# A second late row buffer, another schedule for the late rows, exchanged gate buffers, and second operands split one product later

## The chip, the core and the metric

One core of a Trainium2 chip runs the whole program. The metric is the device time of one execution in microseconds (us); lower is better. The profiled execution has records of every engine: PE (TensorE) for matmuls, PEld for its weight loads, DVE (VectorE), ACT (ScalarE), POOL (GpSimd) and SP (SyncE); SPq stands for the DMA instructions that SP issues.

## The reference, cut to what matters

The reference is one inference step of a decoder layer over 2048 prompt tokens and 8 sample requests. Three kinds of attention (retention, latent attention, attention to a memory) and a gate all take their inputs from one projection, and only that projection is touched here:

```python
def project(h, pos, norm_g, w_in, qnorm_g, w_uq, w_uk, kvnorm_g):
    B, T, _ = h.shape
    z = rms_norm(h, norm_g) @ w_in
    rq, rk, rv, cq, ckv, kpe, mq, gate = _split_cols(z, IN_SIZES)
    rq = rope(rq.reshape(B, T, RET_HEADS, HEAD_DIM), pos)
    rk = rope(rk.reshape(B, T, RET_HEADS, HEAD_DIM), pos) * (HEAD_DIM ** -0.5)
...
```

The hidden width is 1024; `w_in` has 4288 columns, the last 1536 of them the gate's.

## The kernel before

**Stripes and products.** The projection is cut into 15 stripes of `w_in` columns, at most 512 wide (`STRIPES`). Stripes 0 to 8 take the first 1024 tokens (the rows x 0 to 7 of 128 tokens each), stripes 9 to 14 the second 1024 (the eight "late rows"); the gate's columns of the second half come last, in 24 tiles outside the stripes. A stripe is multiplied by a seven-product scheme: x and w are split in quarters, sums and differences of quarters are made, and seven products ("11", "12", "s1", "s2", "s4", "s3", "22") are recombined. Stripes 0 and 10 are narrow and take four products. Each product runs in three passes of fp32r matmuls over a high and a low part of each operand. The products are numbered through as g, from 0 to 98. Stripe 3 begins at g = 18, stripe 4 at 25, stripe 5 at 32, stripe 6 at 39, stripe 7 at 46, stripe 8 at 53, stripe 9 at 60, and the last stripe, 14, at 92. `base` below is 25. Stripes 5 to 8 are of kind "T", products of 24 matmuls of 512 columns.

**Engines.** Every engine runs its own loop over g, written out by hand, and the order inside one g is the order of its instructions. PE: at the last product of a stripe the sample rows' partial products (L1190, `row_parts`), at its second their sum (L1199), then the late rows' transposes (L1087, `late_turn`), then the product (L1162, L1170). ACT: one evacuation of a product at most (L695), the high part of the weights of product g + 2 (L682, `weight_high`, which waits for product g - 1), late rows. DVE: recombination (L902, L1005), the low part of the weights of g + 2 (L868), sums of weights (L880 to L891), rotations (L920 to L927, `rotate`), late rows (L815, L854 to L857). SP issues the stores of results (L494) and the late rows' DMAs; POOL issues the weight loads (L398, L410, L420) and computes the late rows' roots (L388, L390).

**Late rows.** The eight late rows are normalised, transposed and spilled to DRAM during stripes 4 to 8, two to a stripe. For row y: load into the one buffer `row_x` (L474), sum of squares on ACT (L618), root on POOL, scale on DVE (L815), eight transposes in two parts on PE (L1087) into one PSUM bank, each part copied by ACT into `late_x` (L638). PE's second part waits for ACT's copy of the first. After a pair of rows, SP stores four quarters of `late_x` (L477, counted by `late_out`), DVE makes four sums in place (L854 to L857), which waits for `late_out`, and SP stores the four sums (L477, counted by `sums_out`). The copy of the next pair's first part waits for `sums_out`. Only one buffer: the load of the next row waits until the last one is transposed. With p the first product of the pair's stripe, the steps are, for its first row: square at p, scale at p + 1, transposes at p + 2 and p + 3; for its second: load and square at p + 4, scale at p + 5, transposes at p + 6 and p + 7; spill at p + 8, sums at p + 9. The next pair's first row is loaded behind that spill, at p + 8, which is one past the next stripe's first product, where ACT's loop already stands at its square.

```python
def late_turned(y, part):
    act.wait_ge(xT_ps, TURNS + 2 * y + part + 1)
    if y >= 2 and part == 0:
        act.wait_ge(sums_out, 64 * (y // 2))
...
    act.copy(late_x[:, y % 2, part, :, :], turn_bank[0]).then_inc(late_ok, 1)
```

**Second operands.** During stripe 8 and the first product of stripe 9 SP loads the seven operands of the second half, 1 MB each, from DRAM over the old ones, each as soon as stripe 8 has used it (L480); "11" waits for `late_out`, "s1" for `sums_out`. ACT makes the high parts (L661, `second_high`) and DVE the low parts (L848, `low_part`).

**Gate tiles.** For n from 0 to 23 a tile of 24 matmuls (L1211) is copied to `stage` by ACT (even n) or DVE (odd n) and stored by SP. For every four tiles one stripe of gate weights is split by ACT (L692) and DVE (L953, `gate_low`) into `wh` and `wl`. Of the four result buffers c[0] to c[3] of 4 KB each, the stage takes c[0] and c[1] and the second `wl` takes c[2] and c[3]; so `gate_low(1)` waits until the last stripe's results 2 and 3 are stored (`c_out`), and the first copies to the stage until 0 and 1 are. Between the tiles runs the preparation of the sample requests: on DVE `sample.vector(0)` (L3268 to L3274 and L3240 to L3244) stands behind `gate_low(1)`, and PE's `sample.tensor(1)` (L3461, L3465), which stands behind the second tile, waits for it. SP issues the sample's 16 first DMAs (from L3115 on) ahead of the last result store (L494, `store(LAST, 3)`).

Of the kernel before, what the change touches and what calls it, by code (L numbers as in the profile page):

```python
# [21 lines left out]
F32R = mybir.dt.float32r  # L22
# [134 lines left out]

def product_plan():
# [8 lines left out]
    for n, s in enumerate(rotary):  # L167
        for z, after in enumerate((2, 3, 5, 7, 8, 8, 11, 11)):
            pieces.setdefault(first[s] + after, []).append((n, z))
# [4 lines left out]
def project(nc, t, hold, tail):  # L174
# [6 lines left out]
    with ExitStack() as ctx:  # L181
# [37 lines left out]
        row_x = at(right(4 * KB), "row_x", [P, D])  # L219
# [6 lines left out]
        if high.at < low.at:  # L226
# [16 lines left out]
        wl = [at(w_at[1], "wl0", [P, KD, SW], F32R), at(c_at + 8 * KB, "wl1", [P, KD, SW], F32R)]  # L243
        stage = at(c_at, "stage", [P, 2, 2, BIG])
# [6 lines left out]
         gate_out, row_x_in, late_ok, late_out, late_sum, sums_out, chain,  # L251
# [3 lines left out]
            "gate_out row_x_in late_ok late_out late_sum sums_out chain "  # L255
# [7 lines left out]
        op_in = {n: r.sem(f"op_in_{n}") for n in FULL}  # L263
        rope_ok = [r.sem(f"rope_ok{j}") for j in range(2)]
# [44 lines left out]
        def pair_at(j):  # L309

            return first[SPREAD + j]
# [37 lines left out]
        def stage_free(eng, n):  # L349
            if n // 2 >= 2:  # L350
                eng.wait_ge(st_out[n // 2 % 2], 16 * (n // 4))
            else:
                eng.wait_ge(c_out[n // 2], 16 * stored_before(LAST + 1, n // 2))
# [14 lines left out]
        with nc.Block() as block:  # L368
            @block.gpsimd
            def _(pool):  # L370
# [63 lines left out]
                for s in range(len(STRIPES)):  # L434
                    j = s - SPREAD
                    if 0 <= j < LATE_BLOCKS // 2:
                        late_root(2 * j)
                    if 1 <= s < LAST:
                        load_second(s + 1)
                    if 0 <= j < LATE_BLOCKS // 2:  # L440
                        late_root(2 * j + 1)
                    if s + 2 <= LAST:
                        load_first(s + 2)
                load_gate(0)
# [6 lines left out]
            def _(sp):  # L451
# [19 lines left out]
                def load_late(y):  # L471
                    if y:
                        sp.wait_ge(xT_ps, TURNS + 2 * y)
                    sp.dma_start(row_x[:, :], x_rows[KD + 4 * (y % 2) + y // 2]).then_inc(row_x_in, 16)  # L474
# [51 lines left out]
                for g, (s, i) in enumerate(where):  # L526
# [21 lines left out]
                    for n, turned in enumerate(rotary):  # L548
                        for z, after in enumerate((4, 8, 9, 12)):
# [8 lines left out]
                    for j in range(LATE_BLOCKS // 2):  # L558
                        if g == pair_at(j) + 4:
                            load_late(2 * j + 1)  # L560
                        if g == pair_at(j) + 8:
                            sp.wait_ge(late_ok, 4 * j + 4)
                            for a, n in enumerate(("11", "12", "21", "22")):
                                spill(n, j, late_x[:, a // 2, a % 2, :, :]).then_inc(late_out, 16)
                            if j + 1 < LATE_BLOCKS // 2:
                                load_late(2 * j + 2)
                        if g == pair_at(j) + 9:
                            sp.wait_ge(late_sum, j + 1)
                            for n, of in (("s1", late_x[:, 1, 1, :, :]), ("s2", late_x[:, 0, 0, :, :]), ("s4", late_x[:, 0, 1, :, :]),
                                          ("s3", late_x[:, 1, 0, :, :])):  # L570
                                spill(n, j, of).then_inc(sums_out, 16)
# [33 lines left out]
            def _(act):  # L605
# [7 lines left out]
                def late_squared(y):  # L613
                    act.wait_ge(row_x_in, 16 * (y + 1))
# [3 lines left out]
                    act.activation(late_squares[:, :], row_x[:, :], ACT.Square, accum_out=total[:, FRONT + 2 + y:FRONT + 3 + y]).then_inc(sum_ok, 1)  # L618
# [3006 lines left out]
```

## Time and profile before

| | us |
|---|---|
| median of 3 executions | 2212.25 |
| lowest and highest | 2205.29, 2212.87 |
| the profiled execution's own time | 2208.42 |
| its span, first to last instruction | 2206.6 |
| PE busy | 2031.9 (92%) |
| DVE busy | 1447.5 (66%) |
| ACT busy | 764.2 (35%) |
| mean granted TensorE clock, share of full | 0.971 |

Times in rows of the trace are counted from the span's start. The projection up to product 98 ends near 698, the gate tiles near 880, and the attentions and the merge follow. A timeline row is the start, the duration, the engine, the line, the operation with what it writes and reads, and how many were merged in it; in brackets stands how long the engine had sat idle before it and who released it. Matmuls overlap, so a row can end after the next one starts.

### The profile page before, as it was taken

What the parts mean: (1) busy time and instruction counts of PE and PEld (TensorE: products, weight loads), DVE (VectorE), ACT (ScalarE), POOL (GpSimd) and SP (SyncE); (2) the same over time, 40 slices, a digit from 0 to 9 for tenths busy, and PEclk for the clock granted to TensorE, in tenths of its full rate; (3) what the DMA queues carried; (4) which work ended last, traced back from release to release, by engine and by line L of the source; (5) the groups of instructions that cost most, each with busy time, mean ns of one, the idle gap of its engine ahead of it and who ended that gap; (6) DMA issues with size and microseconds to landing.
All of it is one profiled execution on the core that took longest, in us unless ns stands there. A gap on an engine that the chain in (4) does not pass through costs nothing. (4 is left out here: it accounts for less than half of the span.)

```text
span 2206.6 us, 46989 instructions
## 1 busy us (share of the span) xinstructions
PE 2031.9 (92%) x19805; PEld 1711.8 (78%) x19805; DVE 1447.5 (66%) x2517; ACT 764.2 (35%) x1488; POOL 272.5 (12%) x368
## 2 busy tenths in 40 slices
PE   7999988899998789899989999899899999989998
PEld 6899866689996677677767777678788888768886
DVE  3757544464773441898889999677677777655555
ACT  5323322342332111243334333454444545421110
POOL 1000000000000100222222222112302200000000
PEclk9999999999999899899999999899999999999999
DMA  7332444473244663999999999689948542345542
GB/s 241 120 97 78 144 134 134 126 247 101 88 132 152 215 224 144 377 376 369 366 351 386 377 365 374 207 291 347 328 95 167 94 84 99 124 127 161 172 143 86
DMA packets 205013, 454.78 MB, mean 206 GB/s; under 512 B 15328, under 2 KB 114688, under 8 KB 195600
## 3 DMA queue, kind: packets, MB, share of 16 engines
q0 software_dynamic: 49552, 252.12, 34.6%
q1 hardware_dynamic: 155264, 199.81, 27.3%
q8 instruction: 150, 2.46, 0.4%
q14 instruction: 47, 0.39, 0.1%
HBM read 350.00 MB, written 101.69 MB: 205 GB/s over the span
## 5 line engine op out<-in xcount | busy, mean ns | idle before, releaser
L2813 PE MATMUL sa_ps_s<-sa_turned,keep_q 128*32 128x128 f32 x5120 | 184.4, 278 | 26.2 <-DVE sa_turned L2569 21.3
L1170 PE MATMUL pj_ps<-pj_w,pj_xh_s 128*128 128x256 f32 (+1 forms) x1088 | 192.7, 280 | 0.0
L868 DVE TENSOR_TENSOR pj_w<-pj_raw,pj_w 128x1024 fp32r<-128x1024 f32 (+1 forms) x86 | 102.7, 1194 | 119.0 <-ACT pj_w L682 118.8
L1170 PE MATMUL pj_ps<-pj_w,pj_xh 128*128 128x256 f32 (+1 forms) x960 | 173.8, 284 | 3.7 <-DVE pj_kT L862 3.7
L2813 PEld LDWEIGHTS sa_ps_s<-sa_turned,keep_q 128*32 128x32 f32 x5120 | 136.4, 111 | 51.5 <-DVE sa_turned L2569 28.5
L1170 PEld LDWEIGHTS pj_ps<-pj_w,pj_xh_s 128*128 128x128 f32 x1088 | 166.9, 189 | 0.3 <-issue 0.3
L2569 DVE STREAM_TRANSPOSE sa_turned<-sa_nat 128x2048 f32<-128x2048 f32 x64 | 146.9, 2295 | 18.3 <-DMA sa_kp<-cache_kpe,keep_index 18.3
L1170 PEld LDWEIGHTS pj_ps<-pj_w,pj_xh 128*128 128x128 f32 x960 | 150.2, 193 | 9.3 <-issue 5.5
L1170 PE MATMUL pj_ps<-pj_w,pj_xl_s 128*128 128x256 f32 (+1 forms) x544 | 152.4, 280 | 0.0
L2569 DVE STREAM_TRANSPOSE sa_turned<-keep_nat 128x2048 f32<-128x2048 f32 x64 | 146.9, 2295 | 7.6 <-PEq L85 4.8
L1923 DVE TENSOR_TENSOR la_pl<-la_ps_p,la_ph 128x512 fp32r<-128x512 f32 (+1 forms) x144 | 88.4, 657 | 72.1 <-ACT la_ph L1969 72.1
L1170 PE MATMUL pj_ps<-pj_w,pj_xl 128*128 128x256 f32 (+1 forms) x480 | 135.7, 283 | 0.0
L682 ACT CAST pj_w<-pj_raw 128x1024 fp32r<-128x1024 f32 (+1 forms) x86 | 87.9, 1026 | 137.0 <-PE pj_ps L1170 84.1
L1960 ACT ACTIVATE la_row<-la_row,la_soft 128x128 f32<-128x128 f32 (+7 forms) x64 | 77.3, 1208 | 127.6 <-DVE la_soft L1910 127.6
L695 ACT ACTIVATE pj_c<-pj_ps 128x1024 f32<-128x1024 f32 x52 | 53.3, 1026 | 179.5 <-PE pj_ps L1170 97.2
L1162 PE MATMUL pj_ps<-pj_xh_s,pj_w 128*128 128x512 f32 x320 | 108.2, 421 | 2.8 <-ACT pj_c L695 2.8
L1170 PEld LDWEIGHTS pj_ps<-pj_w,pj_xl_s 128*128 128x128 f32 x544 | 102.9, 189 | 0.0
L1902 DVE CUSTOM_DVE_ANT_0 la_row<-la_ps_s,begin_causal 128x512 f32<-128x512 f32 (+3 forms) x160 | 92.2, 605 | 9.2 <-PE la_ps_s L2026 9.2
L1170 PEld LDWEIGHTS pj_ps<-pj_w,pj_xl 128*128 128x128 f32 x480 | 92.9, 194 | 0.0
L1969 ACT CAST la_ph<-la_ps_p 128x512 fp32r<-128x512 f32 (+1 forms) x144 | 74.3, 565 | 39.4 <-PE la_ps_p L2039 38.5
L1162 PEld LDWEIGHTS pj_ps<-pj_xh_s,pj_w 128*128 128x128 f32 x320 | 64.7, 204 | 18.6 <-issue 3.2
L2039 PE MATMUL la_ps_p<-begin_ident,la_row 128*128 128x128 f32 x544 | 74.0, 276 | 4.1 <-DVE la_row L1917 4.1
(516 smaller groups left out, 4995.4 us busy)
## 6 DMA issues: line engine op xcount, KB each, us to landing
pj_raw<-w_in POOLq DMA_DIRECT2D x32, 1024.0 KB, 6.3
s_zn<-pj_c SPq DMA_DIRECT2D x32, 512.0 KB, 2.9
rm_z<-s_zn SPq DMA_DIRECT2D x16, 768.0 KB
s_zt<-pj_c SPq DMA_DIRECT2D x20, 512.0 KB, 2.8
s_x<-pj_late_x SPq DMA_DIRECT2D x32, 256.0 KB
s_k<-lp_st SPq DMA_DIRECT2D x16, 512.0 KB, 8.3
s_v<-lp_st SPq DMA_DIRECT2D x32, 256.0 KB, 4.8
s_qn<-lp_st SPq DMA_DIRECT2D x16, 512.0 KB, 5.5
```

The source lines that it names most:

```text
L682: act.copy(w_parts(g)[0], w_source(s, i)).then_inc(w_hi, 1)
L695: return act.activation(c[:, q, :, :], bank_pair(b), ACT.Copy, scale=factor(s))
L868: dve.tensor_tensor(lo, w_source(s, i), hi, ALU.subtract).then_inc(w_lo, 1)
L1162: mm = pe.matmul(ps[:, bank + u, :], wt[:, b, k, u * P:(u + 1) * P], of[a][:, k, :], start=opens and (k, a, b) == (0, 0, 0), stop=k == HAL ...
L1170: mm = pe.matmul(ps[:, bank + u, x2 * SW:x2 * SW + w], of[a][:, k, rows_at:rows_at + P], wt[:, b, k, 0:w], start=opens and (x2, k, a, b) = ...
L1902: dve.tensor_tensor_reduce(out=row[:, s, q, c * P:(c + w) * P], in0=ps_s[:, (at + n) % 3, 0:w * P], in1=m, scale=1.0, scalar=-3.0e38, op0= ...
L1923: dve.tensor_tensor(pl[:, n % RING, 0:w], ps_p[:, n % RING, 0:w], ph[:, n % RING, 0:w], ALU.subtract).then_inc(pl_ok, 1)
L1960: act.activation(row[:, s, q, 0:n], row[:, s, q, 0:n], ACT.Exp, bias=soft[:, s, q, 1:2], scale=MLA_SCALE, accum_out=soft[:, s, q, 2:3]).th ...
L1969: act.copy(ph[:, n % RING, 0:w], ps_p[:, n % RING, 0:w]).then_inc(ph_ok, 1)
L2039: mm = pe.transpose(ps_p[:, n % RING, at:at + P], of, ident[:, :])
L2569: dve.transpose(turned[:, s, a:z, :, :].rearrange("p c x q -> p x c q"), of.rearrange("p x (c q) -> p x c q", q=QR)).then_inc(t_ok, 1)
L2813: mm = pe.matmul(ps_s[j * QR:(j + 1) * QR, s, 0:TQ * QR], q32[:, u, c, :], turned[:, s, c, j * TQ:(j + 1) * TQ, :].rearrange("p x q -> p ( ...
```

## The change

The late rows get a second buffer, `row_x1`, in 4 KB of the table of rotations; the squares' scratch has the first 2 KB of the same table. Odd rows use it. The first load into it waits until stripe 3's rotations are done, later loads until the row two before is transposed. A function `late_plan()` gives for each row, as distances from product 25, when it is loaded, squared, scaled and first transposed; the second part is transposed one product later. The rows (load, square, scale, transpose) are (0, 0, 2, 3), (4, 6, 7, 8), (5, 9, 10, 12), (10, 11, 12, 14), (14, 15, 16, 18)... in steps of six products per pair: row 4 is (14, 15, 16, 18), row 5 (16, 17, 18, 20), row 6 (20, 21, 22, 24) and row 7 (22, 23, 24, 26). The spills are at 9, 15, 21 and 27, the sums at 10, 16, 22 and 28, where before they were at 8, 15, 22, 29 and 9, 16, 23, 30. Stripe 3's last two pieces of rotation move from 11 products after its first to 9 and 10, and its last store from 12 to 11. POOL's loads and roots are put in order of g. The high parts of the second operands move from 2 to 8 after stripe 8's first product to 3, 4, 6, 7, 8, 9 and 10, and the low parts are one product behind them each. In the gate tiles, the stage and the second `wl` exchange places, and the waits with them. Nothing is computed differently. Blank context and the renaming of the semaphore are left out below, and eight columns of indentation.

```diff
@@ -155,6 +155,17 @@
+def late_plan():
+    plan = [(0, 0, 2, 3), (4, 6, 7, 8)]
+    for j in range(1, LATE_BLOCKS // 2):
+at = 12 + 6 * (j - 1)
+plan.append((5 if j == 1 else at - 4, at - 3, at - 2, at))
+plan.append((10 if j == 1 else at - 2, at - 1, at, at + 2))
+    return plan
...
@@ -165,7 +176,7 @@
-for z, after in enumerate((2, 3, 5, 7, 8, 8, 11, 11)):
+for z, after in enumerate((2, 3, 5, 7, 8, 8) + ((11, 11) if s + 1 in rotary else (9, 10))):
...
@@ -216,7 +227,7 @@
-row_x = at(right(4 * KB), "row_x", [P, D])
+row_x = [at(right(4 * KB), "row_x0", [P, D]), at(rot_at + 2 * KB, "row_x1", [P, D])]
...
@@ -240,19 +251,19 @@
-wl = [at(w_at[1], "wl0", [P, KD, SW], F32R), at(c_at + 8 * KB, "wl1", [P, KD, SW], F32R)]
-stage = at(c_at, "stage", [P, 2, 2, BIG])
+wl = [at(w_at[1], "wl0", [P, KD, SW], F32R), at(c_at, "wl1", [P, KD, SW], F32R)]
+stage = at(c_at + 8 * KB, "stage", [P, 2, 2, BIG])
...
@@ -261,6 +272,7 @@
+row_x_in = [r.sem(f"row_x_in{j}") for j in range(2)]
...
@@ -306,9 +318,18 @@
-def pair_at(j):
-    return first[SPREAD + j]
+late = late_plan()
+base = first[SPREAD]
+late_loaded, late_squares_at, late_scaled, late_turned_at = [{base + x[n]: y for y, x in enumerate(late)} for n in range(4)]
+late_second_at = {g + 1: y for g, y in late_turned_at.items()}
+late_spilled = {g: y // 2 for g, y in late_second_at.items() if y % 2}
+late_summed = {g + 1: j for g, j in late_spilled.items()}
+second_at = {first[SECOND - 1] + after: y for y, after in enumerate((3, 4, 6, 7, 8, 9, 10))}
+def faded_after(n):
+    return (4, 8, 9, 12 if rotary[n] + 1 in rotary else 11)
...
@@ -350,7 +371,7 @@
-        eng.wait_ge(c_out[n // 2], 16 * stored_before(LAST + 1, n // 2))
+        eng.wait_ge(c_out[2 + n // 2], 16 * stored_before(LAST + 1, 2 + n // 2))
...
@@ -431,16 +452,13 @@
-        for s in range(len(STRIPES)):
-            j = s - SPREAD
-            if 0 <= j < LATE_BLOCKS // 2:
-                late_root(2 * j)
-            if 1 <= s < LAST:
+        for g, (s, i) in enumerate(where):
+            if i == 3 and 1 <= s < LAST:
                 load_second(s + 1)
-            if 0 <= j < LATE_BLOCKS // 2:
-                late_root(2 * j + 1)
-            if s + 2 <= LAST:
+            if i == len(names_of(s)) - 1 and s + 2 <= LAST:
                 load_first(s + 2)
+            if g in late_squares_at:
+                late_root(late_squares_at[g])
...
@@ -469,9 +487,11 @@
-            if y:
-                sp.wait_ge(xT_ps, TURNS + 2 * y)
-            sp.dma_start(row_x[:, :], x_rows[KD + 4 * (y % 2) + y // 2]).then_inc(row_x_in, 16)
+            if y == 1:
+                sp.wait_ge(rope_ok[1], 8)
+            elif y >= 2:
+                sp.wait_ge(xT_ps, TURNS + 2 * (y - 1))
+            sp.dma_start(row_x[y % 2][:, :], x_rows[KD + 4 * (y % 2) + y // 2]).then_inc(row_x_in[y % 2], 16)
...
@@ -546,7 +566,7 @@
-                for z, after in enumerate((4, 8, 9, 12)):
+                for z, after in enumerate(faded_after(n)):
...
@@ -555,20 +575,19 @@
-            for j in range(LATE_BLOCKS // 2):
-                if g == pair_at(j) + 4:
-                    load_late(2 * j + 1)
-                if g == pair_at(j) + 8:
-                    sp.wait_ge(late_ok, 4 * j + 4)
-                    for a, n in enumerate(("11", "12", "21", "22")):
-                        spill(n, j, late_x[:, a // 2, a % 2, :, :]).then_inc(late_out, 16)
-                    if j + 1 < LATE_BLOCKS // 2:
-                        load_late(2 * j + 2)
-                if g == pair_at(j) + 9:
-                    sp.wait_ge(late_sum, j + 1)
-                    for n, of in (("s1", late_x[:, 1, 1, :, :]), ("s2", late_x[:, 0, 0, :, :]), ("s4", late_x[:, 0, 1, :, :]),
-                                  ("s3", late_x[:, 1, 0, :, :])):
-                        spill(n, j, of).then_inc(sums_out, 16)
+            if g in late_loaded and late_loaded[g]:
+                load_late(late_loaded[g])
+            if g in late_spilled:
+                j = late_spilled[g]
+                sp.wait_ge(late_ok, 4 * j + 4)
+                for a, n in enumerate(("11", "12", "21", "22")):
+                    spill(n, j, late_x[:, a // 2, a % 2, :, :]).then_inc(late_out, 16)
+            if g in late_summed:
+                j = late_summed[g]
+                sp.wait_ge(late_sum, j + 1)
+                for n, of in (("s1", late_x[:, 1, 1, :, :]), ("s2", late_x[:, 0, 0, :, :]), ("s4", late_x[:, 0, 1, :, :]),
+                              ("s3", late_x[:, 1, 0, :, :])):
+                    spill(n, j, of).then_inc(sums_out, 16)
...
@@ -611,11 +630,11 @@
-            act.wait_ge(row_x_in, 16 * (y + 1))
+            act.wait_ge(row_x_in[y % 2], 16 * (y // 2 + 1))
...
-            act.activation(late_squares[:, :], row_x[:, :], ACT.Square, accum_out=total[:, FRONT + 2 + y:FRONT + 3 + y]).then_inc(sum_ok, 1)
+            act.activation(late_squares[:, :], row_x[y % 2][:, :], ACT.Square, accum_out=total[:, FRONT + 2 + y:FRONT + 3 + y]).then_inc(sum_ok, 1)
...
@@ -760,26 +779,17 @@
-                for z, after in enumerate((4, 8, 9, 12)):
+                for z, after in enumerate(faded_after(n)):
...
-            for j in range(LATE_BLOCKS // 2):
-                if g == pair_at(j) + 7:
-                    late_turned(2 * j + 1, 1)
-            for j in range(LATE_BLOCKS // 2):
-                if g == pair_at(j):
-                    late_squared(2 * j)
-                if g == pair_at(j) + 2:
-                    late_turned(2 * j, 0)
-                if g == pair_at(j) + 3:
-                    late_turned(2 * j, 1)
-                if g == pair_at(j) + 4:
-                    late_squared(2 * j + 1)
-                if g == pair_at(j) + 6:
-                    late_turned(2 * j + 1, 0)
-            if first[SECOND - 1] + 2 <= g < first[SECOND - 1] + 9:
-                y = g - first[SECOND - 1] - 2
-                second_high(FULL[y], y)
+            if g in late_turned_at:
+                late_turned(late_turned_at[g], 0)
+            if g in late_second_at:
+                late_turned(late_second_at[g], 1)
+            if g in late_squares_at:
+                late_squared(late_squares_at[g])
+            if g in second_at:
+                second_high(FULL[second_at[g]], second_at[g])
...
@@ -812,7 +822,7 @@
-            dve.scalar_tensor_tensor(row_x[:, :], row_x[:, :], stat[:, (PAIRS + y) % 2, 1, 0:1], gain[:, :], ALU.mult, ALU.mult)\
+            dve.scalar_tensor_tensor(row_x[y % 2][:, :], row_x[y % 2][:, :], stat[:, (PAIRS + y) % 2, 1, 0:1], gain[:, :], ALU.mult, ALU.mult)\
...
@@ -948,7 +958,7 @@
-                for q in (2, 3):
+                for q in (0, 1):
...
@@ -1031,16 +1041,13 @@
-            for j in range(LATE_BLOCKS // 2):
-                if g == pair_at(j) + 1:
-                    late_scale(2 * j)
-                if g == pair_at(j) + 5:
-                    late_scale(2 * j + 1)
-                if g == pair_at(j) + 9:
-                    late_sums(j)
-            for y, after in enumerate((3, 4, 5, 8, 9, 10, 11)):
-                if g == first[SECOND - 1] + after:
-                    low_part(FULL[y], len(FULL) + y + 1, xr[FULL[y]])
+            if g in late_scaled:
+                late_scale(late_scaled[g])
+            if g in late_summed:
+                late_sums(late_summed[g])
+            if g - 1 in second_at:
+                y = second_at[g - 1]
+                low_part(FULL[y], len(FULL) + y + 1, xr[FULL[y]])
...
@@ -1084,7 +1091,7 @@
-                mm = pe.transpose(turn_bank[0][:, k, :], row_x[:, d:d + P], ident[:, :])
+                mm = pe.transpose(turn_bank[0][:, k, :], row_x[y % 2][:, d:d + P], ident[:, :])
...
@@ -1231,16 +1238,10 @@
-            for j in range(LATE_BLOCKS // 2):
-                if g == pair_at(j) + 7:
-                    late_turn(2 * j + 1, 1)
-            for j in range(LATE_BLOCKS // 2):
-                if g == pair_at(j) + 2:
-                    late_turn(2 * j, 0)
-                if g == pair_at(j) + 3:
-                    late_turn(2 * j, 1)
-                if g == pair_at(j) + 6:
-                    late_turn(2 * j + 1, 0)
+            if g in late_turned_at:
+                late_turn(late_turned_at[g], 0)
+            if g in late_second_at:
+                late_turn(late_second_at[g], 1)
...
```

## Rows read from the trace of the kernel before

**Rows 1.** PE's waits, 225 to 480 us: waited for, us, times, longest.

```profile
PE pj_ps L1087 <- ACT pj_late_x L638: 18.2, 3, 6.9
PE pj_ps L1087 <- DVE pj_row_x L815: 12.0, 4, 3.8
PE pj_ps L1162 <- ACT pj_c L695: 2.8, 1, 2.8
```

**Rows 2.** PE's waits, 697 to 785 us, the same columns.

```profile
PE pj_ps L3461 <- DVE sp_queries L3272: 11.2, 1, 11.2
PE pj_ps L3435 <- DVE sp_weights L3251: 9.2, 1, 9.2
PE pj_ps L3465 <- DVE pj_late_row L3244: 0.6, 1, 0.6
```

**Rows 3.** Windows: stretch, length, busy by engine, PE clock, DMA share, GB/s.

```profile
264.00:478.00 214.00, 183.66 (x827) 141.37 (x826) 98.99 (x93) 63.89 (x73) 11.81 (x20) 0.92 0.50 160
295.00:297.00 2.00, 2.00 (x6) 1.56 (x5) 2.00 (x2) 0.37 (x1) 0.00 (x0) 0.50 0.78 221
659.10:698.00 38.90, 38.88 (x170) 31.38 (x168) 18.58 (x16) 12.72 (x11) 0.89 (x1) 1.00 0.35 122
703.00:713.00 10.00, 7.58 (x34) 5.95 (x32) 0.00 (x0) 0.59 (x1) 0.00 (x0) 1.00 1.04 359
722.00:730.00 8.00, 7.39 (x24) 5.86 (x24) 5.44 (x14) 0.36 (x2) 1.57 (x3) 0.58 0.41 128
```

**Rows 4.** PE's timeline around the late rows, undisturbed steps and the first stall.

```profile
231.75 0.66 PE L1087 MATMUL pj_ps<-pj_ident,pj_row_x 128*128 128x128 f32 x4 [2.69 <-DVE pj_row_x L815]
312.98 1.91 PE L1190 MATMUL pj_ps<-pj_raw,pj_xsT 128*8 128x256 f32 x32
314.82 0.66 PE L1087 MATMUL pj_ps<-pj_ident,pj_row_x 128*128 128x128 f32 x4
315.24 0.71 PE L1162 MATMUL pj_ps<-pj_xh,pj_w 128*128 128x512 f32 x2
326.80 1.02 PE L1199 MATMUL pj_ps<-pj_rows,pj_parts 128*8 128x512 f32 x2
327.76 0.73 PE L1162 MATMUL pj_ps<-pj_xh,pj_w 128*128 128x512 f32 x2
```

**Rows 5.** Timelines of SP, ACT and DVE around the third pair.

```profile
341.90 3.31 SPq L477 DMA_DIRECT2D s_x<-pj_late_x  x4
349.47 0.59 ACT L638 COPY pj_late_x<-pj_ps 128x512 f32<-128x512 f32 x1 [14.73 <-DMA s_x<-pj_late_x]
341.18 0.69 DVE L857 TENSOR_TENSOR pj_late_x<-pj_late_x 128x512 f32<-128x512 f32 x1
330.80 1.06 ACT L618 ACTIVATE pj_late_squares<-pj_row_x 128x1024 bf16<-128x1024 f32 x1 [8.28 <-DMA pj_row_x<-x_prompt]
```

**Rows 6.** DVE timeline ahead of the first transposes: low part, then scale.

```profile
225.05 1.23 DVE L868 TENSOR_TENSOR pj_w<-pj_raw,pj_w 128x1024 fp32r<-128x1024 f32 x1 [3.11 <-ACT pj_w L682]
230.42 1.28 DVE L815 SCALAR_TENSOR_TENSOR pj_row_x<-pj_row_x,pj_stat,pj_gain 128x1024 f32<-128x1024 f32 x1
```

**Rows 7.** Timelines of DVE, PE and SP at the gate tiles.

```profile
699.27 1.22 DVE L902 SCALAR_TENSOR_TENSOR pj_c<-pj_ps,pj_c 128x1024 f32<-128x1024 f32 x1
714.91 2.29 DVE L953 TENSOR_TENSOR pj_wl<-pj_raw,pj_wh 128x2048 fp32r<-128x2048 f32 x1 [14.42 <-DMA s_zt<-pj_c]
721.57 0.47 DVE L3274 SCALAR_TENSOR_TENSOR sp_ckvx<-sp_first,sp_stat,sp_ring 8x256 f32<-8x256 f32 x1
710.20 0.39 PE L1211 MATMUL pj_ps<-pj_xl,pj_wh 128*128 128x512 f32 x1
723.27 0.80 PE L1211 MATMUL pj_ps<-pj_xh,pj_wh 128*128 128x512 f32 x1
706.07 0.43 SPq L494 DMA_DIRECT2D s_zt<-pj_c  x1
731.46 1.18 PE L3472 MATMUL pj_ps<-sp_weights,sp_cqT 128*32 128x192 f32 x24
```

More of the change, by code:

```diff
@@ L250, in project @@
          decay_in, parts_in, rot_in, mm_ok, ev_act, ev_dve, w_hi, w_lo, sum_w, pr_ok, clear_ok, row4_ps, row4_ok, row_ps, row_ok, row_out,
-         gate_out, row_x_in, late_ok, late_out, late_sum, sums_out, chain,
+         gate_out, late_ok, late_out, late_sum, sums_out, chain,
          e1, e2, e3, e4, e5, e6, e7, e7b, p0, p1, g_hi, g_lo, g_ok, g_act, g_dve) = [r.sem(n) for n in (
@@ L254, in project @@
             "decay_in parts_in rot_in mm_ok ev_act ev_dve w_hi w_lo sum_w pr_ok clear_ok row4_ps row4_ok row_ps row_ok row_out "
-            "gate_out row_x_in late_ok late_out late_sum sums_out chain "
+            "gate_out late_ok late_out late_sum sums_out chain "
             "e1 e2 e3 e4 e5 e6 e7 e7b p0 p1 g_hi g_lo g_ok g_act g_dve").split()]
```

## The prediction, made before the change was run

> **What bounds the kernel now.** I read the page first: PE is busy for 92% of the span, so only what makes PE wait, or lowers its clock, can count. Next I read PE's waits in the projection. Between 225 and 480 us PE stands for 33 us, and 30 of it ahead of the late rows' transposes, L1087: 18.2 in three waits for ACT's copy, 12.0 in four for DVE's scale [rows 1]. The window view gives the same from outside: of the 214.0 us of products 32 to 59 PE is busy for 183.66, at a mean granted clock of 0.92, while in the last stripe seven like products take 38.90 at 1.00 [rows 3]. Then the timelines of the engines that PE waits for, to see what they wait for in turn. ACT's copy of a pair's first part idles 14.73 us until SP's stores of the sums have landed, and ACT's square idles 8.28 until the one row buffer is loaded [rows 5]. Both are round trips to DRAM which begin within a product or two of their use, so PE pays. In the gate tiles the same reading gives one long wait, 11.2 us for the sample's queries [rows 2], and behind it DVE, idle for 14.42 until the last store of results lands, ahead of L953 [rows 7].
>
> **The late rows, products 32 to 59.** What would this stretch take without stalls? 28 products at 5.56 (38.90 / 7) are 155.7 [rows 3]. Three times the sample's partial products at 1.84 (314.82 - 312.98) are 5.5, four sums at 0.96 (327.76 - 326.80) are 3.8, and 14 half transposes at 0.42 (315.24 - 314.82) are 5.9 [rows 4]. The sum is 170.9, so 43.1 of the 214.0 are loss: 30.3 idle (214.00 - 183.66), the other 12.8 the lower clock behind the idle times. The clock's part has a row of its own: from 295 to 297, behind one of the stalls, PE runs at 0.50, its 1.2 GHz level [rows 3].
>
> Does the new plan remove the stalls? Take the first pair, with product 34 (base + 9) beginning at 0. PE transposes row 1's second part, ACT makes weights and copies: done at 1.6. SP's four stores take 7.6 from first issue to landing (349.47 - 341.90) [rows 5]. DVE, which now comes to the sums early, waits for them, then needs 2.8 (four like L857, 0.69 each) [rows 5]: 12.0. The second four stores land 7.6 later, at 19.6. Row 2's first copy stands three products later, at 16.7 + 0.8 for transposes + 1 for ACT's weights, 18.5: ACT now idles about 1 us instead of 14.7. PE needs that copy only ahead of product 38, four products on, at 4 x 5.56 + 1.2 = 23.4, and has it at 20.2. So PE doesn't wait, by 3.2 us. The later pairs stand at the same distances, six products apart, and some get 1 to 2 us more from the sample's steps.
>
> The added wait is DVE's. Behind it stands the low part of the weights for product 37, which PE wants at 16.7; DVE is free at 12.0. The row loads now start two or more products, at least 11 us, ahead of their square; the trace shows 8.28 of waiting for one that started too late [rows 5], so these are covered. POOL's weight loads come no later: each stands at the product where its condition is met, and the roots of a few tenths between them wait only for squares just made. Moving the squares, scales and copies costs nothing as long as ACT (63.89 busy of 214) and DVE (98.99) have this room [rows 3]. Issue on SP is unchanged in number; SP waits for the sums from 5.2 to 12.0, and no store of results stands between those two steps; the next is two products on.
>
> The 2.8 us wait of L1162 for ACT [rows 1] comes from ACT standing for a second operand's load. That load now is not queued behind the last stores of the sums and has one product more. I book it as gone; it is inside the 43.1. The extreme values: all of 43.1, or, if each of three pairs keeps half its stall, about 22. I take 42, near the upper end, because the chain above clears PE by 3 us.
>
> **The first transposes** barely gain. The 2.69 us stall at 231.75 [rows 4] moves one product on, but DVE now also makes a rotation ahead of the scale. DVE's work goes on at 230.42 [rows 6] with a combination (1.22), the sample's rows (about 0.7), a low part (1.23), a rotation (about 2.1, half of what lies between the low part and L815) and the scale (1.28): 236.9. PE is ready at 229.06 + 5.56 = 234.6. A stall of 2.2 is left; gain 0.5, between 0 and 2.7.
>
> **The gate tiles.** `gate_low(1)` no longer waits for the store that SP issues last, at 706.07 [rows 7], but for the last stripe's first two, which stand at its third and sixth product. DVE goes on at 700.5 (699.27 + 1.22) instead of 714.91. From there the chain to the sample's second vector is 7.1 (721.57 + 0.47 - 714.91) plus 0.8 for its last row, 7.9: done at 708.4, while PE gets there at 710.6 [rows 7]. Gone are 11.2 and 0.6 [rows 2] and the clock behind them: the third tile takes 8.19 (731.46 - 723.27) [rows 7] at a mean of 0.58 [rows 3], where 5.56 would do, 2.6 more. Together 14.4. The bounds: 0 if the sample's inputs land later than 710, since no row shows when they do; 14.4 otherwise. They are the first five of SP's issues and are on their way before the gate's weights; I take 14.4. The stage's second copy of each engine now waits for the last store, whose landing released L953 at 714.91 [rows 7]; it is wanted near 717. The 9.2 us wait at L3435 [rows 2] hangs on copies that SP issues after a tile of PE's, so it moves along and stays.
>
> One DMA is pulled forward: POOL's load of the fourth gate stripe, 1 MB, from 717 to 703, into a stretch where the DMA engines are full (1.04, 359 GB/s) [rows 3]. It adds 1 / 0.359 = 2.9 us to whatever is outstanding: the last store then lands near 718 and delays one copy to the stage by 1, nothing on PE. The Trainium skill ("DMA: Bandwidth & Descriptors", Issuing engines are not separate DMA queues) says that transfers started by different engines interleave on the same 16 DMA engines; by it the sample's inputs could be slowed as well, which is the third rival below.
>
> The same page (Anatomy of one DMA) fits a transfer by about 2.0 us plus bytes over 436 GB/s. By it four stores of 256 KB would be 4.4 us, an estimate, where the row has 7.6; the pairs' chain would clear PE by 9 us, and the sum would stay.
>
> **The sum.** 42 + 0.5 + 14.4 = 56.9. Against the profiled execution's 2208.4 that is 2151.5. The median of the runs shown stands 3.8 above that execution and the lowest 3.1 below, so I take 2153.
>
> **Rivals.** (1) *The stores' round trip ends last again.* PE is clear while two round trips and the sums fit: each may grow by half of 3.2, to 9.2. Loads of weights and rows fall into the same products, and DMA shares of 0.78 occur there [rows 3]. At 11 us each, PE waits 2 x 1.8 per pair, and with 2 us of lower clock that is 5.6 for three pairs, 17: 2170. (2) *Slower.* The same mechanism carried on, in the same place: to be slower by over 0.5%, 68 us must be given back, 23 per pair, which needs round trips near 20 us. There DVE's wait also holds the weights' low parts. At 21 us: 3 x (2 x 11.8 + 2) = 77, 2229. Nothing in the trace comes near it: 7.6 was the longest of three. (3) *The gate's gain is lost*, because the sample's inputs land late or because what moves earlier only waits longer at L3435, if its data and not PE sets that point: 14.4 back, 2167. For it: the full DMA engines. Against: the order of issue. (4) *The plan does not do what it says*: another step of the late rows stalls ahead of each pair and the product's pace stays; with the gate's part failing too this is no change, 2205.
>
> **How the numbers follow.** Forecast 0.66; rival 1 0.15; rival 3 0.13; rival 4 0.04; slower 0.02. About 0.5%, 11 us, is what a measurement of this kernel can tell from no change. Faster: 0.66 + 0.15 + 0.13 = 0.94; same 0.04; slower 0.02. The range runs from 2138, if the stall at L3435 should shrink too and a run falls on the low side, to 2176, rival 1 in full with some of rival 3.
>
> **What would show it.** Right: PE's waits at L1087 fall from 30 us to under 4, the stretch from product 32 to 59 takes about 172 at a clock of 0.99 or more, DVE's L848 for "12" comes without PE's wait at L1162; L953 starts near 700.5 less 42, and L3461 follows the second tile at once; L3435 keeps 9. Wrong: ACT's L638 idling over 5 us for the stores, DVE idling for `late_out` with PE behind it, or a new wait at L3461 for a DMA.

## The result, and the profile after

The changed kernel takes 2157.55 us, the median of four executions (2155.99 to 2163.47), against 2210.6 (2205.29 to 2212.87): a ratio of 0.9768, 95% interval 0.9742 to 0.9795. Forecast were 2153.0 and the range 2138 to 2176. The profiled execution took 2158.46, its span is 2156.7, and the span of before was 2206.6: 49.9 us less. In two of the experiments below one execution fell far out (6386 us with the late rows alone, 2850 with the pairs five products apart); their times are the medians of the other three.

The late rows first. Three views of the profile after: PE's waits from 225 to 440 us, PE's timeline (the two waits, then the rows at which product 32 and product 60 begin), and the windows of the stretch between.

```profile
PE pj_ps L1094 <- ACT pj_late_x L657: 2.3, 1, 2.3
PE pj_ps L1094 <- DVE pj_row_x L825: 2.2, 1, 2.2
```

```profile
237.58 0.66 PE L1094 MATMUL pj_ps<-pj_ident,pj_row_x 128*128 128x128 f32 x4 [2.20 <-DVE pj_row_x L825]
264.80 0.63 PE L1169 MATMUL pj_ps<-pj_xh,pj_w 128*128 128x512 f32 x2
304.72 0.63 PE L1094 MATMUL pj_ps<-pj_ident,pj_row_x 128*128 128x128 f32 x4 [2.29 <-ACT pj_late_x L657]
438.50 0.40 PE L1177 MATMUL pj_ps<-pj_w,pj_xh 128*128 128x256 f32 x2
```

```profile
264.80:438.50 173.70, 171.41 (x834) 133.82 (x833) 97.53 (x92) 62.90 (x73) 15.81 (x20) 1.00 0.62 195
279.00:291.00 12.00, 12.00 (x54) 9.74 (x53) 5.02 (x6) 4.97 (x7) 1.79 (x3) 1.00 0.87 260
294.00:302.00 8.00, 8.00 (x59) 5.79 (x61) 4.42 (x4) 1.05 (x1) 2.33 (x2) 1.00 0.84 231
```

(L1087 of before is L1094 now, L638 is L657, L815 is L825.) Of 33 us of waiting [rows 1] 4.5 are left. Products 32 to 59 take 438.50 - 264.80 = 173.7 us instead of 214.0, and PE is busy for 171.41 of them at a clock of 1.00, where it was 0.92 [rows 3]. What is left in the stretch is one wait, 2.29 us at the first pair. Its cause is read from the timelines of SP, DVE, ACT and POOL there:

```profile
279.65 3.06 SPq L497 DMA_DIRECT2D s_x<-pj_late_x  x4
290.96 0.69 DVE L864 TENSOR_TENSOR pj_late_x<-pj_late_x 128x512 f32<-128x512 f32 x1 [1.84 <-DMA s_x<-pj_late_x]
293.85 3.19 SPq L497 DMA_DIRECT2D s_x<-pj_late_x  x4
303.99 0.59 ACT L657 COPY pj_late_x<-pj_ps 128x512 f32<-128x512 f32 x1 [8.35 <-DMA s_x<-pj_late_x]
281.06 0.95 POOL L431 DMA_DIRECT2D pj_raw<-w_in  x1
295.39 0.95 POOL L419 DMA_DIRECT2D pj_raw<-w_in  x1
337.84 0.59 ACT L657 COPY pj_late_x<-pj_ps 128x512 f32<-128x512 f32 x1 [0.95 <-DMA s_x<-pj_late_x]
```

The first pair's two round trips take 290.96 - 279.65 = 11.3 and 303.99 - 293.85 = 10.1 us, where the prediction had 7.6 each. Into both fall 1 MB loads of weights by POOL, and the DMA engines are at 0.87 and 0.84. The later pairs fare better: ACT waits 0.95 us in the second (337.84), not at all after it, and PE never.

The gate tiles. PE's waits from 600 to 800 us; the timelines of DVE, PE, SP and ACT; one window of the same stretch:

```profile
PE pj_ps L3436 <- DVE sp_weights L3252: 10.0, 2, 9.2
...
```

```profile
660.92 2.28 DVE L963 TENSOR_TENSOR pj_wl<-pj_raw,pj_wh 128x2048 fp32r<-128x2048 f32 x1
659.92 0.50 PE L1218 MATMUL pj_ps<-pj_xh,pj_wh 128*128 128x512 f32 x1 [1.43 <-DVE pj_wl L963]
671.05 0.35 PE L3462 MATMUL pj_ps<-keep_ident,sp_queries 8*128 8x8 f32 x3
671.51 0.50 PE L1218 MATMUL pj_ps<-pj_xh,pj_wh 128*128 128x512 f32 x1
677.18 1.02 PE L3473 MATMUL pj_ps<-sp_weights,sp_cqT 128*32 128x192 f32 x20
663.50 0.88 POOL L441 DMA_DIRECT2D pj_raw<-w_in  x1 [1.25 <-DVE pj_wl L963]
667.43 0.46 SPq L514 DMA_DIRECT2D s_zt<-pj_c  x1
678.72 0.59 ACT L804 COPY pj_stage<-pj_ps 128x512 f32<-128x512 f32 x1 [6.92 <-DMA s_zt<-pj_c]
```

```profile
671.00:678.00 7.00, 7.00 (x51) 5.55 (x54) 2.54 (x5) 0.31 (x2) 0.00 (x0) 1.00 1.05 383
```

The 11.2 us wait for the queries [rows 2] isn't in the list any more: the low part L963 follows straight on the combination, the transposes of the queries follow straight on the second tile, and the third takes 677.18 - 671.51 = 5.67 us instead of 8.19, at a clock of 1.00 instead of 0.58. The last store now holds up ACT's copy to the stage, until 678.72, with nobody behind it. The wait of 9.2 for `sp_weights` stays.

Behind the gate tiles, one row of each kernel: the sample attention's first product of scores and its last, before and after.

```profile
L2813 PE MATMUL sa_ps_s<-sa_turned,keep_q x5120: 269/273/421, 888.3 to 1406.8; 128*32 128x128 f32 x197
L2814 PE MATMUL sa_ps_s<-sa_turned,keep_q x5120: 269/273/423, 831.8 to 1355.9; 128*32 128x128 f32 x197
```

It begins 56.5 us earlier and ends 50.9 earlier: 5.6 us are given back in a stage that the diff doesn't touch (518.5, then 524.1).

### The profile page after: what moved, and what is told of

Same layout as the page of the kernel before. It is cut to its first block and busy times, and to the rows that moved or that the text cites. A ratio compares the mean times of both kernels' runs of the same rounds, so it can differ in the third digit from the quotient of the medians.

```text
span 2156.7 us, 46989 instructions
## 1 busy us (share of the span) xinstructions
PE 2015.5 (93%) x19805; PEld 1697.7 (79%) x19805; DVE 1447.6 (67%) x2517; ACT 762.7 (35%) x1488; POOL 277.9 (13%) x368
## 5 line engine op out<-in xcount | busy, mean ns | idle before, releaser
L1169 PE MATMUL pj_ps<-pj_xh_s,pj_w 128*128 128x512 f32 x320 | 100.7, 396 | 0.0
L912 DVE SCALAR_TENSOR_TENSOR pj_c<-pj_ps,pj_c 128x1024 f32<-128x1024 f32 x39 | 47.7, 1222 | 51.4 <-PE pj_ps L1177 28.7
```

What stands on the lines that cost most here:

```text
L1169: mm = pe.matmul(ps[:, bank + u, :], wt[:, b, k, u * P:(u + 1) * P], of[a][:, k, :], start=opens and (k, a, b) == (0, 0, 0), stop=k == HAL ...
```

## The experiments

**The gate's exchange alone**: the kernel before, with the edit below.

```diff
-wl = [..., at(c_at + 8 * KB, "wl1", [P, KD, SW], F32R)]
-stage = at(c_at, "stage", [P, 2, 2, BIG])
+wl = [..., at(c_at, "wl1", [P, KD, SW], F32R)]
+stage = at(c_at + 8 * KB, "stage", [P, 2, 2, BIG])
...
-eng.wait_ge(c_out[n // 2], ...)
+eng.wait_ge(c_out[2 + n // 2], ...)
...
-for q in (2, 3):
+for q in (0, 1):
```

> The kernel before with the exchange of the stage and the second wl alone. Theory (the parts add up, and the exchange takes away one DVE wait): L953 starts at about 700.5 instead of 714.91, L3461 follows the second tile without a wait, the third tile runs at full clock; 14 to 16.5 us less than before, about 2195, with the late rows' seven PE waits (30 us) as they were. Rival (the freed time only makes the wait at L3435 longer, from 9.2 to over 20): under 5 us less. Second rival (the gain of the whole change in this stretch leans on the late rows' gain): under 8 us less.

Measured: 2195.24 us, ratio 0.9929 (0.9905 to 0.9954) to the kernel before, 2212.24 in the same session. The longest of its waits from 655 to 790 us; none is at L3461:

```profile
PE pj_ps L3435 <- DVE sp_weights L3251: 9.0, 1, 9.0
...
```

0.0071 of 2212 is 15.7 us, 10 to 21 by the interval: the gate's part stands by itself and has the size of its term, 14.4. PE's timeline has it more closely. From the first tile to the end of the third this kernel takes 715.01 - 697.78 = 17.2 us, as the changed one does (677.18 - 659.92), against 32.05 before. The wait at L3435 did not grow, so the first rival falls, and the second with it.

**The late rows alone**: the changed kernel with the same exchange taken back.

> The changed kernel with the stage and the second wl back in their old places; the late rows, second operands and rotations stay changed. Theory (additive): products 32 to 59 take 173 to 175 us, the gate tiles keep the 11.2 us wait at L3461 and its clock: 14 to 16.5 us more than the changed kernel, about 2173. Rival (the two parts interact, because the earlier stores leave the DMA engines freer at the gate tiles): less than 8 us more than the changed kernel.

Measured: 2174.67 us, ratio 0.9831 (0.9779 to 0.9882), so 0.0169 of 2212, 37.4 us. Its waits have the gate's one back, and the late rows' stay away:

```profile
PE pj_ps L1094 <- ACT pj_late_x L657: 3.0, 1, 3.0
...
PE pj_ps L3462 <- DVE sp_queries L3273: 10.7, 1, 10.7
```

15.7 and 37.4 make 53.1, against 2210.6 - 2157.55 = 53.05 for both: the two parts add. That the sums agree to a tenth is luck, since the intervals of the parts are 10 to 21 and 26 to 49 us. Products 32 to 59 take 439.23 - 263.15 = 176.1 us here, by PE's timeline, against 214.05 before. The run is 17 us longer than the changed kernel, where 14 to 16.5 were expected, so its rival (under 8) falls.

**The second buffer without the new schedule**: the kernel before, with the row loads moved forward as far as a second buffer allows, and all other steps as they were.

```diff
-row_x = at(right(4 * KB), "row_x", [P, D])
+row_x = [at(right(4 * KB), "row_x0", [P, D]), at(rot_at + 2 * KB, "row_x1", [P, D])]
...
-if g == pair_at(j) + 4:
+if g == pair_at(j) + (4 if j == 0 else 1):
     load_late(2 * j + 1)
+if g == pair_at(j) + 5 and j + 1 < LATE_BLOCKS // 2:
+    load_late(2 * j + 2)
```

> The kernel before with the second row buffer alone (and the earlier last two rotations of stripe 3 that it needs): the rows are loaded as soon as their buffer is free, but squared, scaled, transposed, spilled and summed at the old products. Theory (the two round trips of the stores bound the distance from a pair's spill to the next pair's first copy, and the row's load is a second wait inside the same time): ACT's 8.3 us waits for the row load go, PE's waits for DVE's scale (2.7 to 3.9 us) go, and PE's waits for ACT's copy grow from 5.2 to 6.9 to about 8 to 9 each; total 0 to 4 us less than before. Rival (each wait has its own price): PE's waits for the scale and their clock go for good, 12 to 18 us less, about 2195.

Measured: 2203.46 us, ratio 0.9966 (0.9942 to 0.9991), 7.5 us. PE's waits from 225 to 480 us:

```profile
PE pj_ps L1091 <- ACT pj_late_x L642: 21.4, 3, 7.2
PE pj_ps L1091 <- DVE pj_row_x L819: 2.9, 1, 2.9
```

Three of the four waits for the scale are gone, 9.1 us, and the copies' wait, which stands behind them in each pair, takes 3.2 of that back (18.2 [rows 1], now 21.4). The 7.5 us lie between what the theory (0 to 4) and the rival (12 to 18) expected: the copies' waits did grow, but to 7.1 or 7.2 each and not to 8 or 9. So an earlier load is worth something, but not the large part of the 37 us. In this kernel, as before, a pair's sums and the next pair's first copy stand in the same product; in the changed schedule there are two products between them, and with it the copies' waits fall from 21.4 to 3.0 (the run above). That this distance is what gives the other 30 us is the difference of two runs, which differ in the other steps of the schedule as well; no run changes the distance alone from none to two.

**Pairs five products apart**, not six: the changed kernel with one number less. One product instead of two is left between a pair's sums and the next pair's first copy.

```diff
-at = 12 + 6 * (j - 1)
+at = 11 + 5 * (j - 1)
```

> The changed kernel with the pairs one product closer: the first copy of a pair one product after the last pair's sums instead of two (the plan's distances 12 + 6 (j - 1) become 11 + 5 (j - 1)). Theory (the round trips end last once the distance is a product shorter): in the changed kernel the first pair overran by 2.3 us and the second cleared PE by about 2.3, so here PE waits for ACT's copy three times, about 8 us at the first pair and 2 to 5 at the others, and with 1.5 to 2 us of lower clock each the run is 12 to 22 us longer than the changed kernel. Rival (it was the second buffer and the earlier loads that freed PE, the distance has room): under 4 us longer.

Measured: 2162.65 us, ratio 0.9772 (0.9716 to 0.9827). PE's waits for the copies there, ACT's timeline with the first copy of the second, third and fourth pair, and the timelines of SP and POOL at the first of them:

```profile
PE pj_ps L1094 <- ACT pj_late_x L657: 6.4, 3, 5.0
```

```profile
299.58 0.58 ACT L657 COPY pj_late_x<-pj_ps 128x512 f32<-128x512 f32 x1 [4.21 <-DMA s_x<-pj_late_x]
334.22 0.59 ACT L657 COPY pj_late_x<-pj_ps 128x512 f32<-128x512 f32 x1 [4.56 <-DMA s_x<-pj_late_x]
367.81 0.58 ACT L657 COPY pj_late_x<-pj_ps 128x512 f32<-128x512 f32 x1 [6.11 <-DMA s_x<-pj_late_x]
294.12 2.61 SPq L497 DMA_DIRECT2D s_x<-pj_late_x  x4
297.06 0.95 POOL L419 DMA_DIRECT2D pj_raw<-w_in  x1 [2.29 <-DVE pj_w L878]
```

With one product less the round trip comes last in all three pairs, as the chain of the prediction has it: ACT idles 4 to 6 us each time. PE loses less than was expected, 6.4 us in waits of 5.0, 0.3 and 1.0, and the median's distance to the changed kernel, 5 us, is inside both intervals. Products 32 to 59 take 445.01 - 265.16 = 179.9 us, against 173.7 and, in the repeat below, 177.5. The kind is right, the size was put too high, and one reason can be read: the second round trip takes 299.58 - 294.12 = 5.5 us here, and 5.4 at both later pairs (328.82 to 334.22, 362.37 to 367.81), where the changed kernel's first pair has 10.1.

**The changed kernel again**, as the level for three more.

> The changed kernel once more, as it stands. It serves as the level for the other three, and it shows how much one stage that the change doesn't touch scatters: the sample attention, which took 518.5 us before and 524.1 after. Theory (scatter): this profile shows a length anywhere between 518 and 527, and a median near 2158. Rival (the change itself costs 5.6 us there, by where the stage begins): again 523.5 to 524.5.

Measured: 2159.12 us (2153.62 to 2167.28), ratio 0.9782 (0.9756 to 0.9808) to 2210.81. PE's wait for ACT's copy was 4.6 us here, not 2.3: the same four stores took 306.38 - 294.20 = 12.2 us, not 10.1, and products 32 to 59 took 442.41 - 264.87 = 177.5 us, not 173.7. The sample attention took 521.0 us (first row); it took 526.5 with the gate's exchange alone (second row), whose start lies between those of before and after:

```profile
L2814 PE MATMUL sa_ps_s<-sa_turned,keep_q x5120: 269/273/422, 835.0 to 1356.0; 128*32 128x128 f32 x197
L2813 PE MATMUL sa_ps_s<-sa_turned,keep_q x5120: 269/273/423, 870.3 to 1396.8; 128*32 128x128 f32 x197
```

Over the ten profiles of this study the stage took 518 to 527 us, in no order of its start. The same kernel, profiled twice, differs by 3.1. The seven profiles with the gate's exchange have 519.0 to 526.5, the three without it 518.2, 518.5 and 521.6. Its windows, before and after, show what it leans on:

```profile
888.00:1407.00 519.00, 478.87 (x10298) 374.45 (x10302) 468.90 (x688) 198.99 (x641) 139.51 (x168) 0.99 0.97 370
831.00:1356.00 525.00, 476.69 (x10295) 369.74 (x10299) 469.60 (x688) 197.93 (x641) 139.75 (x169) 0.98 0.95 365
```

PE's work is the same, and the DMA engines are at 0.95 to 0.97 throughout. So most of the 5.6 us may be scatter between profiled executions; a cost of the exchange of 2 or 3 us can't be told from it with ten profiles.

**Row 3's load one product later**, behind the stores of the sums.

```diff
-plan.append((10 if j == 1 else at - 2, at - 1, at, at + 2))
+plan.append((11, 12, 13, 14) if j == 1 else (at - 2, at - 1, at, at + 2))
```

> Only row 3's load moves back, by one product, behind the first pair's stores of the sums on SyncE's queue, with its square and scale one product later. Theory: that 1 MB load is what stretched the first pair's first four stores to 11.3 us (the second pair's took 8.5 at most); they take 8 to 9 here, ScalarE's copy idles 2 to 3 us less, and TensorE's wait of 2.29 goes to 0: 2155 to 2157. Rival: GpSimd's weight load, which was issued just before it, is the one that counts, or the second four stores now share with the row load instead: TensorE still waits over 1.5 us there.

Measured: 2154.86 us, ratio 0.9758 (0.973 to 0.9786), not to be told from the changed kernel's. The timelines of SP, DVE, ACT, POOL and PE:

```profile
279.11 3.10 SPq L497 DMA_DIRECT2D s_x<-pj_late_x  x4
290.69 0.69 DVE L864 TENSOR_TENSOR pj_late_x<-pj_late_x 128x512 f32<-128x512 f32 x1 [2.12 <-DMA s_x<-pj_late_x]
293.59 3.46 SPq L497 DMA_DIRECT2D s_x<-pj_late_x  x4
297.09 0.66 SPq L494 DMA_DIRECT2D pj_row_x<-x_prompt  x1
299.93 0.58 ACT L657 COPY pj_late_x<-pj_ps 128x512 f32<-128x512 f32 x1 [4.83 <-DMA s_x<-pj_late_x]
280.52 0.95 POOL L431 DMA_DIRECT2D pj_raw<-w_in  x1
304.11 0.95 POOL L419 DMA_DIRECT2D pj_raw<-w_in  x1
310.73 0.66 PE L1094 MATMUL pj_ps<-pj_ident,pj_row_x 128*128 128x128 f32 x4 [2.81 <-DVE pj_row_x L825]
```

The first round trip takes 290.69 - 279.11 = 11.6 us though the row's load (512 KB, not the 1 MB that the expectation gave it) no longer falls into it: the load wasn't the cause. The second shrank to 299.93 - 293.59 = 6.3, and what left that stretch is the weights' load, issued at 304.11 instead of 295.39, because on POOL's queue it stands behind row 3's root, which waits for the square. Four profiles have that load 1.5 us behind the first of the four stores: the changed kernel and its repeat, the late rows alone, and the run below. The stores took 10.1, 12.2, 10.7 and 11.5 us there. With the pairs five apart the load came 2.9 us behind, and they took 5.5. So of the theory's conclusion (ACT's wait goes) one half came true by another route, and PE got a new wait of 2.81 for row 3's scale instead.

**The second operands split as early as before**, the rest changed.

```diff
-second_at = {first[SECOND - 1] + after: y for y, after in enumerate((3, 4, 6, 7, 8, 9, 10))}
+second_at = {first[SECOND - 1] + after: y for y, after in enumerate((2, 3, 4, 5, 6, 7, 8))}
...
-if g - 1 in second_at:
-    y = second_at[g - 1]
-    low_part(FULL[y], len(FULL) + y + 1, xr[FULL[y]])
+for y, after in enumerate((3, 4, 5, 8, 9, 10, 11)):
+    if g == first[SECOND - 1] + after:
+        low_part(FULL[y], len(FULL) + y + 1, xr[FULL[y]])
```

> The second operands' high and low parts go back to their old products (2 to 8, and 3, 4, 5, 8 to 11 after the stripe's start); the rest is as changed. Theory: splitting them later is worth the 2.8 us wait at the transfer of c, since the operands' loads are issued behind the last pair's stores: that wait is back at 2 to 4 us and the median is 2160 to 2162. Rival: with the sums stored earlier the loads land in time anyway; no wait over 0.5 us there, and no difference from 2158.

Measured: 2157.01 us, ratio 0.9759 (0.9732 to 0.9787). PE's waits from 225 to 480 us have no line for `pj_c`:

```profile
PE pj_ps L1094 <- ACT pj_late_x L657: 3.9, 1, 3.9
PE pj_ps L1094 <- DVE pj_row_x L825: 2.4, 1, 2.4
```

The rival holds: the later split is worth nothing that shows. What is left as the cause for the end of the 2.8 us wait [rows 1] is that the last sums are stored earlier, and the operands' loads behind them on SP with them. This is by elimination; no run has the old stores with the later split.

**Both remaining waits**: the first pair's second row one product earlier, and on DVE the late row's scale ahead of the rotations.

```diff
-plan = [(0, 0, 2, 3), (4, 6, 7, 8)]
+plan = [(0, 0, 2, 3), (4, 5, 6, 7)]
...
+if g in late_scaled:
+    late_scale(late_scaled[g])
 for n, y in pieces.get(g, ()):
     rotate(n, y)
-if g in late_scaled:
-    late_scale(late_scaled[g])
```

> Rows 0 and 1: the first pair's row 1 is loaded, squared, scaled and transposed one or two products earlier, and the scale stands ahead of the rotations on VectorE. Theory: both waits that are left go, 2.20 us at the first transposes and 2.29 at the first pair's ScalarE copy, with perhaps 1 us of clock: 3 to 5 us, a median of 2153 to 2155. Rival: the rotations, pushed back by the scale, make the next product's weights late, or the store chain only shifts, so the waits reappear under other names: 2157 to 2160.

Measured: 2152.93 us (2144.55 to 2154.39), ratio 0.9735 (0.9712 to 0.9758): 6.2 us under the changed kernel's median in the same session, with intervals that still overlap by 0.0002. The list of PE's waits between 225 and 440 us is empty. Its window, the timelines of SP and DVE at the first pair, and PE's rows at which products 32 and 60 begin:

```profile
264.00:438.00 174.00, 174.00 (x861) 136.74 (x860) 99.13 (x94) 64.13 (x73) 16.05 (x20) 1.00 0.64 203
```

```profile
270.62 2.71 SPq L497 DMA_DIRECT2D s_x<-pj_late_x  x4
277.96 0.67 DVE L864 TENSOR_TENSOR pj_late_x<-pj_late_x 128x512 f32<-128x512 f32 x1
262.35 0.71 PE L1169 MATMUL pj_ps<-pj_xh,pj_w 128*128 128x512 f32 x2
433.39 0.40 PE L1177 MATMUL pj_ps<-pj_w,pj_xh 128*128 128x256 f32 x2
```

DVE finds the first four stores landed at 277.96, within 7.3 us of their issue; they now go out ahead of the stripe's store of results (276.34) and of POOL's load (279.73). The stretch from product 32 to 60 takes 433.39 - 262.35 = 171.0 us, and the prediction's count for it without any stall was 170.9, with one half transpose more. The run has two edits; each is read at its own place, the scale's at the first transposes, ahead of product 32, and the row's at the first pair.

## Why the prediction was right, and where it was off

Step by step, on the profiled executions (2151.5 forecast, 2158.46 measured, 7.0 apart):

- **Late rows, 42 booked, 40.4 measured.** The repeat of the same kernel has 36.5 (214.05 - 177.54), so the closeness of this one owes something to luck. The mechanism held: the scale's waits go with the earlier loads (the two-buffer experiment), the copies' with the new schedule, and they begin to come back when its distance is cut. The term mis-sized is the round trip. "SP's four stores take 7.6 from first issue to landing" and "So PE doesn't wait, by 3.2 us" hold for the second pair (7.1 us from 330.72 to 337.84) and not for the first, with 11.3 and 10.1; the two together are 6.2 us over. SP also issued the first of them 0.8 late, at 279.65, 2.4 and not 1.6 behind product 34's start at 277.28, since two other stores stood ahead of it. Against these 7.0 us stood the 3.2 that were spare and 1.8 by which PE came to product 38 later than counted (25.2 behind product 34's start, not 23.4, with the sample's partial products in between); PE's wait of 2.29 is what is left, within 0.3. That is rival 1 in one pair of three, for 2.3 us of its 17, and 4.6 in the repeat. The row of 7.6 is from a kernel that moves 160 GB/s in this stretch [rows 3]; the changed one moves 195, and 260 at the first pair. The Trainium skill ("DMA: Bandwidth & Descriptors", Issuing engines are not separate DMA queues) has transfers of different engines interleave on the same 16 DMA engines; the trace agrees here: four 256 KB stores took 6.3 us without POOL's load beside them and 10.1 with it. The same page's fit made four such stores 4.4 us, an estimate; the page gives that fit for transfers that GpSimd issues, and these are SyncE's. The quickest of the trips read here took 5.4.
- **Second operands.** The prediction gave two causes for the end of the 2.8 us wait; the one run that parts them leaves the earlier stores, by elimination.
- **First transposes, 0.5 booked.** The wait forecast as 2.2 is 2.20, by the steps given. But product 32 begins 0.9 us later than before (264.80, 263.94), so that the term is -0.9, outside the bounds of 0 and 2.7. What the term left out is the clock. The windows from 229 to 247 us, after and before:

```profile
229.00:247.00 18.00, 15.80 (x122) 15.59 (x121) 12.64 (x19) 6.26 (x8) 0.94 (x1) 0.91 0.42 132
229.00:247.00 18.00, 15.31 (x130) 15.25 (x130) 8.48 (x11) 8.02 (x10) 0.94 (x1) 1.00 0.46 147
```

  Behind the stall of 2.20 the granted clock falls, to 0.57 from 238 to 242, and the product there takes 245.32 - 237.99 = 7.3 us. With the late rows alone the stall is 2.35 at the same place, the clock stays at 1.00, the product takes 5.8, and product 32 begins at 263.15. So 1.5 us are the clock's, and it doesn't fall every time: it stayed at 1.00 behind the longer stall of 2.69 before. Half a microsecond more was already lost when product 27 began, and about 0.8 was gained, unbooked, by two half transposes that now stand behind product 32's start.
- **Gate tiles, 14.4 booked, 14.8 measured** (from the first tile to the end of the third 731.46 - 699.41 = 32.05 before and 677.18 - 659.92 = 17.26 after), and the rest of the stage 2.2 shorter still, of which nothing was booked; its clock is 0.95 after and 0.93 before, and one wait for a copy to the stage is 1.0 instead of 1.9. L963 was to start near 700.5 less the late rows' gain, and does at 660.92, 39.6 earlier than 700.5; `sp_ckvx` is done at 668.04 by DVE's timeline, 3 us ahead of its use, so rival 3 fails. POOL's load moved forward and delays one copy to the stage, as told, and nothing on PE.
- **Behind it** nothing was booked, and this execution gave back 5.6 in the sample attention and 1.0 later: that is 6.6 of the 7.0, much of it scatter by the ten profiles. The repeat gave back less there, 2.5 and 0.7, and had less at the late rows, so that its span, 2156.5, is nearly the same: the parts scatter by 3 or 4 us each and cancel. The sum of the terms as measured: 40.4 - 0.9 + 17.0 - 5.6 - 1.0 = 49.9, the difference of the spans.

Against the medians the forecast is 4.6 us low, 0.2%, closer than its parts deserve. Rival 2 (slower) never came near: the longest round trip read in any profile was 12.2 us, the first pair's second in the repeat. Rival 4 is ruled out by PE's waits.

## What to carry to other kernels

When a wait for a store's landing is planned away, take the landing time not from the row in the stalled kernel but from the busiest stretch into which the new pace will put it, and leave that much room: here 7.6 us became 10 to 12 where a 1 MB load fell beside it. Moving the first pair's step by one product emptied the list of waits; shortening one of its round trips only exchanged one wait for another. What a distance is worth depends on how much is there already: with none left between a pair's sums and the next copy PE waited 7 us a pair, with one product 5.0, 0.3 and 1.0, with two 2.3 or 4.6 in the first pair alone. A term for a stall needs one for the clock behind it, which may come or not: here 1.5 us turned a small gain into a loss. And before a few microseconds given back in a late, DMA-bound stage are blamed on a change, run the same kernel again: here that stage differed by 3.1 us between two profiles of one kernel, and by 8 over ten profiles.

## What the runs showed that was not expected

The order on an engine that only issues DMAs matters for contention as much as the issue times planned: moving row 3's square by one product moved a 1 MB load of weights on POOL's queue by 8.7 us (295.39 to 304.11), since it stands behind that row's root, and this changed the landing of SP's stores from 10.1 to 6.3 us. Little is needed: in the run with pairs five apart the same load went out 2.9 us behind the first store instead of 1.5, and the stores took 5.5. What slows the first round trip, POOL's load at 280.5 or the stripe's own store of results just ahead of it on SP, was not parted: both left the stretch together when the pair moved.
